# Thirty-two tokens instead of sixteen leave the dense expert products, and GpSimd makes 41 weight remainders a layer

## The reference

```python
u = jnp.take(expert_u, ic, axis=0)
a = jnp.einsum('cd,chkd->chk', hc, u)
w = gc * jax.nn.gelu(a, approximate=False)
return jnp.einsum('chk,chkd->cd', w, jnp.take(expert_v, ic, axis=0))
```

## Time and profile before

| | |
|---|---|
| three runs | 2772.82, 2774.80 and 2775.05 us, median 2774.8 us |
| profiled execution, its own time | 2772.15 us |
| its span, first to last instruction | 2770.4 us |
| busy | PE 2693.1 us (97%), DVE 2127.9 us (77%), ACT 1381.1 us (50%), POOL 382.7 us (14%) |
| chain that ended last | PE 84%, DVE 8%, ACT 3% |
| DMA | 574.34 MB, mean 207 GB/s |

### The profile page before, as it was taken

One profiled execution on the slowest core, in us unless ns is written; L12 is line 12 of the kernel. 1 busy time (PEld: TensorE's weight loads), 2 busy tenths in 40 slices (PEclk: granted clock), 3 DMA queues, 4 the chain that ended last, 5 costly groups with the idle time before them and its releaser, 6 DMA issues.

```text
span 2770.4 us, 39894 instructions
## 1 busy us (share of the span) xinstructions
PE 2693.1 (97%) x16254; PEld 2321.3 (84%) x16254; DVE 2127.9 (77%) x3176; ACT 1381.1 (50%) x1632; POOL 382.7 (14%) x294
## 2 busy tenths in 40 slices
PE   7999999999999999999999999999999999999998
PEld 6778888788888888998888888897889988788887
DVE  7787887775555579989978777646699989888776
ACT  4645446554455455554444344464555554434443
POOL 0210002000023001122102012040011222002121
PEclk8999999999999999999999999999999999999999
DMA  8757876466553355555456588644555655456785
GB/s 312 268 198 296 313 257 225 155 213 197 190 199 129 135 190 191 205 198 170 166 183 212 185 290 295 225 150 139 165 180 197 209 182 176 149 198 218 258 289 185
DMA packets 86470, 574.34 MB, mean 207 GB/s; under 512 B 9840, under 2 KB 10352, under 8 KB 23056
## 3 DMA queue, kind: packets, MB, share of 16 engines
q1 hardware_dynamic: 75888, 534.86, 55.1%
q0 software_dynamic: 10400, 36.93, 3.8%
HBM read 563.32 MB, written 8.44 MB: 206 GB/s over the span
## 4 chain that ended last, share of the span: by engine, by line
PE 84%; DVE 8%; ACT 3%; issue 3%; DMA 1%; POOL 1%; SPq 0%; POOLq 0%; DVEq 0%; ACTq 0%
PE banks L492 22%; PE banks L499 11%; PE banks L590 11%; PE banks L592 10%; PE banks L600 10%; DVE wlo L1610 3%; PE banks L564 2%; PE banks L566 2%; PE banks L575 2%; ACT whi L1095 2%; PE banks L1030 2%; PE banks L534 1%; PE banks L536 1%; PE banks L546 1%; PE banks L630 1%
## 5 line engine op out<-in xcount | busy, mean ns | idle before, releaser
L1095 ACT ACTIVATE whi<-raw 128x2048 fp32r<-128x2048 f32 x438 | 839.7, 1917 | 962.6 <-issue 761.7
L1610 DVE TENSOR_TENSOR wlo<-raw,whi 128x2048 fp32r<-128x2048 f32 x422 | 977.0, 2315 | 240.6 <-ACT whi L1095 239.8
L492 PE MATMUL banks<-ht,whi 128*128 128x480 f32 (+1 forms) x2848 | 675.1, 387 | 5.9 <-DVE big L1708 3.4
L492 PEld LDWEIGHTS banks<-ht,whi 128*128 128x128 f32 x2848 | 524.0, 190 | 88.9 <-issue 3.6
L590 PE MATMUL banks<-whi,ht 128*128 128x512 f32 x1152 | 454.5, 395 | 10.4 <-DVE ht L1698 10.4
L592 PE MATMUL banks<-whi,ht 128*128 128x512 f32 x1152 | 449.8, 390 | 0.0
L499 PEld LDWEIGHTS banks<-ht,wlo 128*128 128x128 f32 x2848 | 351.7, 190 | 11.4
L499 PE MATMUL banks<-ht,wlo 128*128 128x240 f32 (+1 forms) x2848 | 354.0, 277 | 0.0
L600 PE MATMUL banks<-wlo,ht 128*128 128x512 f32 x1152 | 288.8, 390 | 2.1 <-DVE wlo L1610 2.1
L590 PEld LDWEIGHTS banks<-whi,ht 128*128 128x128 f32 x1152 | 216.9, 188 | 56.5 <-issue 12.1
L600 PEld LDWEIGHTS banks<-wlo,ht 128*128 128x128 f32 x1152 | 216.7, 188 | 47.9 <-DVE wlo L1610 3.0
(11 more groups left out here) (311 smaller groups left out, 3579.1 us busy)
## 6 DMA issues: line engine op xcount, KB each, us to landing
raw<-in_pu SPq DMA_DIRECT2D x128, 1024.0 KB, 4.9
raw<-in_pv SPq DMA_DIRECT2D x128, 1024.0 KB, 4.9
raw<-in_win SPq DMA_DIRECT2D x52, 1024.0 KB, 4.9
big<-in_wmod SPq DMA_DIRECT2D x28, 1024.0 KB, 7.1
raw<-in_wgate SPq DMA_DIRECT2D x22, 1024.0 KB, 6.4
raw<-in_wup SPq DMA_DIRECT2D x22, 1024.0 KB, 5.7
raw<-in_wdown SPq DMA_DIRECT2D x22, 1024.0 KB, 5.0
raw<-in_wmod SPq DMA_DIRECT2D x20, 1024.0 KB, 5.1
```

The source lines that it names most:

```text
L492: m = e.matmul(wide(b + n, t), h[:, q, c[n]], x[:, q], start=q == 0, stop=False, skip_group_check=True)
L1095: e.activation(whi(j), slot[u][0], ACT.Copy).then_inc(*hi.mark(j))
L1610: e.tensor_tensor(wlo(j), slot[u][0], whi(j).bitcast(F32), ALU.subtract).then_inc(*lo.mark(j))
```

## The change

FEW goes from 16 to 32, so NT goes from 240 to 224 and the gate groups from 30 to 28 for each half. 64 tiles are gathered for each layer instead of 32. Their DVE work moves to units 9 to 34 (dots) and 37 to 61 (additions) of pv. The buffers of the ring and the operands move to places that the smaller dense array leaves free. The first gate groups start after unit 32 instead of 36, two in each odd unit of pu and none in the even ones, and the late drain moves to unit 63. POOL makes 41 remainders for each layer instead of 8: twelve in pu during the selection, fifteen at the odd units 33 to 61 of pu, and fourteen in pv.

```diff
-GATES = 36
-FEW = 16
+GATES = 32
+FEW = 32
-POOLED = (37, 40, 43, 46, 49, 52, 55, 58)
+POOLED = (), (3, 5), (8, 10), (13, 15), (18, 20), (22, 24), (27, 29), (), tuple(range(33, 62, 2))
+POOLED_V = (1, 3, 5, *range(10, 31, 2))
...
     def pace(u):
-        return 2 if u % 16 == 1 else 1
+        return 2 if u % 2 else 0
...
     def dots_due(v):
-        return 1 if 31 <= v < 47 else 0
+        return 0 if not 9 <= v < 35 else 2 if v % 4 == 2 and v < 34 else 1
 
     def adds_due(v):
-        return 0 if v < 48 or v > 60 else 2 if v % 4 == 1 else 1
+        return 0 if v < 37 or v > 61 else 2 if v % 4 == 1 else 1
...
-                due = plan.step(pace(u))[0] if GATES < u < 61 else []
+                due = plan.step(pace(u))[0] if GATES < u < 63 else []
...
-                    some(2.2)
+                    some(2.5)
...
+        def remainder(j):
+            on.wait_ge(*hi.at(j))
+            on.wait_ge(*unit.at(j - NSP))
+            e.tensor_tensor(wlo(j), slot[place_of[j]][0], whi(j).bitcast(F32), ALU.subtract).then_inc(*p_lo.mark(j))
...
+                if h < 7:
+                    for u in POOLED[h]:
+                        remainder(first["pu", l] + u)
...
+            asked = 0
+            for v in range(64):
+                if v + 1 in POOLED_V:
+                    remainder(first["pv", l] + v + 1)
+                if v == DENSE:
+                    on.wait_ge(*part_lo.at(("w", l, DENSE)))
+                    ids(l)
+                    gathered(l, 0)
+                    gathered(l, 1)
+                if v == DENSE_ROWS:
+                    gathered(l, 2)
+                    gathered(l, 3)
+                    asked = RINGS
+                if v >= DENSE_ROWS:
+                    while asked < min(2 * FEW, RINGS + sum(dots_due(x) + adds_due(x) for x in range(v + 1))):
+                        gathered(l, asked)
+                        asked += 1
```

More of the change, by code:

```diff
@@ L202, in program @@
     HT = Halves(at("ht", 57344, 2 * UN, F32R)[:, :])
-    OH = [[at(f"oh0{i}", 73728 + 4 * (29696 + 1024 * i), 2048, F16) for i in range(3)],
+    OH = [[at(f"oh0{i}", 73728 + 4 * (28672 + 1024 * i), 2048, F16) for i in range(3)],
           [at("oh1a", 65536, 2048, F16), at("oh1b", 65536 + 4096, 2048, F16)]]
@@ L284, in program @@
     E1, E2, RP, II, SS = 27136, 29184, 31232, 31744, 32512
-    HREP, ACC, ROWS_OF, PICK = 2048, 3072, 4096, 4096 + 1024 * RINGS
+    HREP, ACC, PICK = 28672, 29696, 2048
+    ROWS_OF = 30720, 31744, 2560, 3584
     SLOTS, IDU, IDV, DOTS, IDF, IDC = (PICK + 128 + FEW * i for i in (0, 3, 4, 5, 6, 7))
-    DENSE = -(-(IDC + FEW) // (2 * NT)) - 1
+    DENSE, DENSE_ROWS = -(-ROWS_OF[2] // (2 * NT)) - 1, -(-(ROWS_OF[3] + 1024) // (2 * NT)) - 1
     def gcols(l, i):
@@ L354, in program @@
     few_ids = [nc.dram_tensor(f"fewi{l}", [FEW, 3 * P], F32, kind="Internal").ap() for l in range(DEPTH)]
-    pooled = {first["pu", l] + u for l in range(DEPTH) for u in POOLED}
+    pooled = {first["pu", l] + u for l in range(DEPTH) for us in POOLED for u in us}
+    pooled |= {first["pv", l] + v for l in range(DEPTH) for v in POOLED_V}
     def low_at(k):
@@ L416, in region @@
             on.wait_ge(*d_ids.at(l))
-        if u >= 61:
+        if u >= 63:
             on.wait_ge(*took_v.at(("hot", l, 0, NG - 1)))
@@ L1041, in peer @@
                         m.then_inc(*turned.mark(("top", l, t)))
-                if u == 61:
+                if u == 63:
                     while plan.left():
@@ L1569, in peer @@
                     split_weights(v + 1)
-                if v == 48:
+                if v == 36:
                     on.wait_ge(*few.at((l, "dot", FEW - 1)))
@@ L2317, in peer @@
                     slots_turned(l, 1)
-                if GATES < u < 61:
+                if GATES < u < 63:
                     gate_step(l, 0, *plan.step(pace(u)))
                 if u < GATES - 2:
-                    some(2.2)
+                    some(2.5)
             def split_weights(v):
@@ L2329, in row @@
                 on.wait_ge(*d_row[r].at((l, m)))
-                return ag(ROWS_OF + 1024 * r, 1024)
+                return ag(ROWS_OF[r], 1024)
             def dot(n):
@@ L2603, in ids @@
             e.tensor_tensor(ag(HREP, 1024), ag(HREP, 1024), ag(ACC, 1024), ALU.mult).then_inc(*p_rep.mark(l))
+        def remainder(j):
+            on.wait_ge(*hi.at(j))
+            on.wait_ge(*unit.at(j - NSP))
+            e.tensor_tensor(wlo(j), slot[place_of[j]][0], whi(j).bitcast(F32), ALU.subtract).then_inc(*p_lo.mark(j))
         def gathered(l, m):
             r, n = m % RINGS, m % FEW
+            if m in (2, 3):
+                on.wait_ge(*part_lo.at(("w", l, DENSE_ROWS)))
             if m >= RINGS:
@@ L2611, in gathered @@
             on.wait_ge(*p_ids.at((l, "v")))
-            e.indirect_dma_start(ag(ROWS_OF + 1024 * r, 1024), None, table,
+            e.indirect_dma_start(ag(ROWS_OF[r], 1024), None, table,
                                  bass.IndirectOffsetOnAxis(ag(at_ + n, 1).bitcast(U32), 0)).then_inc(*d_row[r].mark((l, m)))
@@ L2632, in peer @@
                             AG[P - FEW:P, o:o + P].rearrange("t (s n) -> t s n", s=SUB)).then_inc(*d_ids.mark(l))
-            for u in POOLED:
-                j = first["pu", l] + u
-                on.wait_ge(*hi.at(j))
-                on.wait_ge(*unit.at(j - NSP))
-                e.tensor_tensor(wlo(j), slot[place_of[j]][0], whi(j).bitcast(F32), ALU.subtract).then_inc(*p_lo.mark(j))
+            for u in POOLED[8]:
+                remainder(first["pu", l] + u)
             on.wait_ge(*row_free.at((l, 63, 3)))
@@ L2641, in peer @@
             on.wait_ge(*d_few.at(l))
-            on.wait_ge(*part_lo.at(("w", l, DENSE)))
-            ids(l)
-            for m in range(2 * FEW):
-                gathered(l, m)
+            asked = 0
[15 more added lines that the diff above has]
+                        asked += 1
         inverse(("m", 0), 1)
```

## The result

The changed kernel takes 2795.76 us (median of four runs, 2793.94 to 2803.5) against 2773.99 us before: ratio 1.0084, 95% interval 1.0064 to 1.0104, so 22 us slower where 145 were predicted. The profiled execution's span is 2793.1 us.

The account below looks back on a forecast made before the run. PE, busy 97% of the span, was taken as the bound. Against 2772.15 us, -63.0 + 112 + 39 + 9 + 48 = +145 gave 2917 us, as a median 2920 us; range 2800 to 2960.

Parts of the forecast that it names:

- (1): High and low matmuls of pu get fewer columns, 0.31 us a unit saved over 128 units: -39.7 us.
- (3): All gate groups of pu made by unit 59, so no drain and no slow pass behind it: -19.0 us.
- (2): Two gate groups fewer in each half, eight in all at 0.54 us of PE each: -4.3 us.
- pu's gate pairs: POOL's remainder gets into DVE's second gate group in pu; PE waits 4.0 us in 28 pairs: +112 us.
- (4): PE's clock falls after each 4.0 us wait in pu, 1.4 us each for 28 waits: +39 us.
- (5): Twelve POOL remainders during pu's selection relieve DVE but block its two-input operations: nothing booked, up to 10 us a layer.
- (6): POOL remainders of pv units 1, 3 and 5 delay gate groups PE wants first: 4.5 us a layer, +9 us.
- (7): Dots beside gates from pv unit 9: DVE's 10.8 plus POOL's 4.6 us exceed PE's 11.95 a pair: +48 us.
- (8): DMA in pv, 1.70 MB in 5.44 us a unit, 313 GB/s, engines about 89% busy: hidden, nothing booked.
- (b): Rival: all pu pairs escape POOL's hold, needing POOL 0.7 us later or groups earlier, pv doesn't: 2769 us, chance 0.05.
- (c): Rival: POOL waits for DVE's whole run to end; no pu waits, pv remainders in gaps: 2712 us, chance 0.11.

Follow-up runs that it names:

- few16: The kernel before (16 tokens, pv untouched) with the changed kernel's pu schedule of gates and POOL remainders; 2754.03 us, ratio 0.9917 to the kernel before.
- pu_runs: The changed kernel with three and one gate groups in turn in pu's odd units instead of two and two; 2808.18 us.
- pu_break: On top of pu_runs, where three groups stand, `joined`, which reads PSUM, is moved between the second and the third; 2859.15 us.
- quarters: The changed kernel with every POOL remainder of the expert layers in four instructions of 512 columns instead of one of 2048; 2822.3 us.
- pv_gap: The changed kernel, each POOL remainder of pv from unit 10 on also waiting until the last gather asked for ahead of it has landed; 2847.63 us.
- no_sel: v_none without the twelve POOL remainders during the selection in pu; the fifteen of the gate part stay; 2749.11 us.
- v_start: The changed kernel with POOL remainders in pv at units 1, 3 and 5 alone; 2749.29 us.
- v_none: The changed kernel with no POOL remainder in pv, DVE making all 64; 2739.17 us.
- best: v_none with dots spread over units 9 to 36, additions in 38 to 60, and the remainder of pu's unit 35 on DVE; 2723.6 us.
- rem_first: The changed kernel with POOL remainders of pv, but the first, one place further up, ahead of unit v's gathers instead of behind them; 2802.3 us.

## Why the prediction was wrong

The direction was right and the size was not. By its own terms:

- **(1) fewer columns, -39.7 us: mis-sized.** A unit saved 5.27 - 5.05 = 0.22 us, so 128 units are -28 us. The high pass shrank as counted. The low pass did not: the 0.11 us read between 256 and 240 columns does not come again between 240 and 224. A passage from one pair of rows was taken for a slope.
- **(3) no drain, -19.0 us: right.** few16, which has (3) and the remainders of pu, but not (1) and (2), is 20.0 us faster. **(2) fewer groups, -4.3 us,** was tried by no run alone.
- **pu's gate pairs, +112 us: the step that failed.** "So POOL gets in between two operations of a running group and the rest of the group waits." The place and the phase were right (O + 5.4, second operation of the second group). So was the price of a pair in which it happens: 5.5 us measured, 4.0 + 1.4 booked. How often it happens was wrong: once, not 28 times. In 27 of 28 pairs, and in 13 of 14 of pu_runs with longer runs, POOL waited until DVE reached an operation that reads PSUM. pu_break shows the other half: with such an operation amid the gates POOL takes its chance each time. The earlier trace rows were one instance in each layer, and a row ahead of them in the kernel before was not read:

```profile
1507.65 2.14 POOL L2600 CAST big<-big 128x16 uint32<-128x16 f32 x1
```

Its record ends 0.05 us after DVE's `wlo` (1507.43 + 2.31), for which it seems to have waited, and the multiply of the earlier trace rows follows directly on it. In the pairs of pu POOL comes out of idleness. Whether that is the difference was not tried by itself; quarters and pv_gap say that it is not the whole of it. Why went the other way stays open.

- **(4) the clock, +39 us: fell with it.** Its price for one wait was about right: 1.6 us behind the one wait of 3.76 us, 1.1 us at the high matmuls behind the waits in pu_break, with 1.4 booked. Elsewhere in the gate stretch there was no wait and no lower clock (1.00 from 1225 to 1370). In pv, where PE did wait, the granted clock was 0.94 over the stretch, and the prediction had booked nothing there.
- **(5) the selection, 0: right within 1.2 us a layer.** From unit 0 to unit 32 of pu the profile has 166.9 us, 5.8 less than before, where 32 x 0.22 = 7.0 would be PE's own gain. Without POOL's twelve remainders the same stretch takes 8.3 us a layer more (no_sel).
- **(6) the start of pv, +9 us: right in size** (10.1 us, v_start against v_none), though by unit 1 alone and with the clock's fall, instead of three small waits.
- **(7) the dots, +48 us: right.** 46.5 us by v_start; the rows give 28.1 us a layer, of which v_none keeps 4.6. The rule behind it, that DVE and POOL add up wherever DVE has only port operations, held in the table above to 0.6 us a pair. Who goes first changed the rows, and not the sum.
- **(8) DMA: hidden**, as booked. The additions at unit 61 cost 1.0 us a layer (8.25 instead of 7.21 us between units 61 and 62; best, which ends them at 60, has 7.21).

The outcome is that of rival (b), pu escapes and pv pays, which had 2769 us and a chance of 0.05. Its reason is not what happened: it wanted POOL 0.7 us later, and POOL asked where the forecast had put it. The reason is that of rival (c), which had pu right and pv wrong: it was priced as one case, 2712 us, as if POOL's habit had to be the same in both phases. With pu from (c) and pv from the forecast the terms, as measured and (2) as booked, are -20.0 - 28 - 4.3 + 10.1 + 46.5 = +4.3; the single pair caught in pu adds some 5, unit 61 2, and the dots on DVE alone 2 x 4.6 = 9: +20.5, against 21.8 measured, which is closer than the terms are known. (b)'s outcome for (c)'s reason should have had a larger chance.

The Trainium skill ("SBUF — State Buffer", SBUF: two separate sides) says that whichever of the two operations starts first gets the pair for the whole instruction. The rows agree on the exclusive hold (every blocked operation ends after POOL's does), and differ on who gets it. In pu POOL asked at 1225.82, and DVE's operations of 1226.02 and 1226.36 went ahead of it; in pv the dot at 1456.09 and the split at 1470.46 began before POOL's remainder and ended after it. The rows decide.

## What to carry to other kernels

Where two engines share a port, first add up what both hold it over a period of the bound engine. Above the period the sum sets the pace and the order changed little (rem_first), so a remainder moved to POOL costs 4.6 us and gives 2.3 back. Below the period the order decides whether anything is lost. In a gate pair of pu the sum is 2.3 (`wlo`) + 3.2 (two groups) + 4.6 = 10.1 of 11.13 us, and yet one PSUM operation amid the gates cost 51 us in pu_break, and the one remainder ahead of the first gates of pv some 5 us a layer. So look at what breaks the first engine's run, and keep operations that read PSUM out of a group that must not be held up. And a step that multiplies one observed instance by 28 needs a chance of its own for that instance being special.

## What the runs showed of the hardware

- POOL, asking from idle amid a run of DVE's operations with two inputs in SBUF, waited until DVE came to one that reads PSUM, past up to six further ones (2.5 us). It got in early in a few cases: some of those in which it asked 0.12 to 0.16 us into L2256, and once at 0.47 us. What tells these apart stays open.
- Once in, with short instructions, POOL and DVE took turns in the pu gate pairs of quarters; but a DVE operation that began during the last 0.1 to 0.4 us of a POOL gather was passed over by everything that POOL had queued, four instructions included.
- In rem_first POOL was served where a dot ended, though another dot stood next on DVE (5.63 instead of 1.22 us).
- A low pass of 16 matmuls takes 1.94 us with 224 columns and 1.96 us with 240.
- After a wait of 3.76 us PE's granted clock was 0.62 over the next 3 us (changed kernel), after waits of 1.41 and 2.53 us in one unit 0.50 over 3 us (pu_break).
